# The last expert round of a sparse mixture-of-experts kernel, written out behind its loop

## The chip, the cores and the metric

The kernel is one program on one NeuronCore of a Trainium2 chip. Times are microseconds of device time for one launch; of several runs the median is taken. The engines are TensorE (PE; its weight loads are PEld), VectorE (DVE), ScalarE (ACT), GpSimd (POOL) and SyncE (SP, which here only starts DMA transfers).

## The reference

The network is a trunk of two layers on 1024 tokens of width 1024. A layer is a token mixer (a spatial gating unit in layer 0, a pooling mixer in layer 1) and a mixture of 32 experts with SwiGLU. Each token goes to two experts. Only the expert part matters here:

```python
def expert_block(args):
    xb, e = args                               # 128 gathered token rows, one expert
    hid = jax.nn.silu(xb @ w_gate[e]) * (xb @ w_up[e])
    return hid @ w_down[e]
...
w_sorted = gate.reshape(-1)[order]
out = jax.ops.segment_sum(y_sorted * w_sorted[:, None], tok, num_segments=n_tok)
```

`w_gate` and `w_up` of an expert are 1024x512, `w_down` is 512x1024, all float32.

## The kernel before

The expert part, `moe(L)` on every engine, runs once per layer over n items. An item is one expert with at most 128 of its tokens; n is read from a table in the middle of the run, and is 32 or 33 here. Every float32 operand is split in a high part (`w_hi`, `a_hi`, made by ACT with a copy) and a low part (`w_lo`, `a_lo`, made by DVE with a subtraction), and a product is three matmuls: high by high, high by low, low by high (`three`, L525 to L527).

A **round** i of the loop on PE is `round_(i)` (L744 on): the gate and up products of item i (`gate_up`, 8 units of 6 matmuls, banks 0 and 1), the 8 transposes of the token rows of item i+1 (`x_transposes`, L709, banks 4 and 5), the down product of item i-1 (`down`, 4 units of 6 matmuls, banks 2 and 3), and the 4 transposes of item i's inner rows (`h_transposes`, L742, bank 6). So the down product runs one round late. A unit is 128x1024 of weights: ACT splits it (L844), DVE makes its low part (L1154), and there are four slots for split units, each free again when PE has used it (`M.used`).

On ACT a round is: four units, the weighted rows of item i-2 out of banks 2 and 3 into `y_sb` (`y_out`, L1025), the high part of the inner rows of item i-1 (`h_split`), four units, the SiLU (L1015), four units of the down weights, and the high part of the next token rows (`x_split`). DVE follows in the same order; its `hidden` (L1504) makes SiLU(gate) times up, the input of `h_transposes`.

On POOL a round is: `gather(i+1)`, which loads the 128 list entries of the next item (`meta_g`) and gathers its token rows into `xg`; `scatter(i-2)`, which writes the weighted rows to `y_rows` in DRAM and waits until they have landed; and `load_meta(i-1)`, which loads the entries that the next `y_out` and scatter need (`meta_s`).

The loop runs to round n-1, whatever is left to gather: in its last round a spare gather and spare transposes for an item n are made, which nobody uses. Behind the loop stands the down product of the last item. It waits (L772) until ACT has emptied banks 2 and 3 of the item before, and then, in `down`, until the split inner rows are there; these are made behind that emptying on ACT. POOL then scatters item n-2, loads the entries of item n-1, and scatters it. SP waits for all scatters and gathers (L346, L347) and loads `y_rows` back, two rows per token in 8 transfers (L352). DVE adds each pair of rows to the residual (L1179, L1181) and normalizes it (L1162).

The loop of ACT and DVE starts at round 3, that of PE and POOL at round 2. The down weights of the last item are loaded early into their own place (`early_raw`, semaphore `g.last_dn`).

## Time and profile before

| what | us |
|---|---|
| median of 3 runs | 2170.41 |
| lowest, highest run | 2161.85, 2173.72 |
| span of the profiled execution | 2153.2 |
| TensorE busy in it | 2007.8 (93%) |

The span reaches from the first to the last instruction. In the views, L followed by a number is a line of the kernel; "x4" after an instruction is a count of equal ones merged; "[3.16 <-DVE a_lo L1154]" says that the engine had stood idle for 3.16 us and that the DVE instruction of L1154 ended it. A matmul of 512 columns shows as 0.39 us but the next starts 0.23 us after it, since they are pipelined.

### The profile page before, as it was taken

The page shows a single profiled execution, that of the slowest core. Times are in us where ns is not written, and L with a number is a line of the kernel's source. Part 1 is how long each engine was busy: PE and PEld are TensorE (multiplying, and loading weights), DVE is VectorE, ACT ScalarE, POOL GpSimd, SP SyncE. Part 2 cuts the span into 40 slices and gives each one's busy share as a digit, 9 for nine tenths or more (in the row PEclk, how much of TensorE's full clock was granted, in tenths as well). Part 3 has the DMA queues.
Part 4 walks back from the last instruction along what each step waited for, and adds up shares of the span by engine and source line. Part 5 has one row for each costly group of instructions (what it writes and reads, how often), then busy time and mean ns, then how long its engine had stood idle before and what let it go on. Part 6 is the DMA issues. An engine that isn't in the chain of part 4 may idle for free.

```text
span 2153.2 us, 31966 instructions
## 1 busy us (share of the span) xinstructions
PE 2007.8 (93%) x9518; PEld 1672.5 (78%) x9518; DVE 1581.8 (73%) x1894; ACT 1365.6 (63%) x1742; POOL 283.4 (13%) x319
## 2 busy tenths in 40 slices
PE   7999999999969999999999879898799999999991
PEld 6887778888858888888887658687588888888871
DVE  4335353426479999999998786757799999999985
ACT  3442244433248888888888743434588888888872
POOL 1000000000031211112222100001212222221110
PEclk9999999999979999999999979999899999999995
DMA  7332222322478999999999663144889999999976
GB/s 278 98 98 68 89 85 95 99 97 80 163 203 308 381 380 384 386 384 372 379 383 364 236 243 95 66 147 134 265 332 377 378 381 383 376 376 387 391 282 251
DMA packets 165860, 553.13 MB, mean 257 GB/s; under 512 B 31525, under 2 KB 33797, under 8 KB 163632
## 3 DMA queue, kind: packets, MB, share of 16 engines
q1 hardware_dynamic: 138624, 507.57, 64.0%
q0 software_dynamic: 25840, 39.95, 5.3%
q10 hardware_dynamic: 1344, 4.94, 0.6%
q8 instruction: 30, 0.49, 0.1%
q14 instruction: 22, 0.18, 0.0%
HBM read 539.85 MB, written 47.78 MB: 273 GB/s over the span
## 4 chain that ended last, share of the span: by engine, by line
PE 71%; DMA 14%; DVE 6%; issue 4%; ACT 2%; POOL 1%; POOLq 1%; SPq 0%; ACTq 0%; DVEq 0%
PE bank L525 22%; PE bank L527 22%; PE bank L526 22%; DMA y_rows<-big,metas 7%; DMA metas<-lists 5%; PE bank L709 2%; PE bank L584 2%; DVE big L1162 1%; DMA lists<-payload,place 1%; PE bank L742 1%; POOLq L461 1%; POOL lists L453 1%; PE bank L623 1%; PE bank L573 1%; DVE w_lo L1154 1%
## 5 line engine op out<-in xcount | busy, mean ns | idle before, releaser
L525 PE MATMUL bank<-w_hi,a_hi 128*128 128x512 f32 x1816 | 725.9, 400 | 17.6 <-DVE a_lo L1154 12.6
L1154 DVE TENSOR_TENSOR w_lo<-raw,w_hi 128x1024 fp32r<-128x1024 f32 x376 | 458.6, 1225 | 356.8 <-ACT w_hi L844 334.7
L527 PE MATMUL bank<-w_hi,a_lo 128*128 128x512 f32 x1816 | 713.6, 393 | 0.0
L526 PE MATMUL bank<-w_lo,a_hi 128*128 128x512 f32 x1816 | 711.4, 392 | 0.0
L844 ACT ACTIVATE w_hi<-raw 128x1024 fp32r<-128x1024 f32 x376 | 397.3, 1060 | 415.2 <-PE bank L527 407.9
L1154 DVE TENSOR_TENSOR w_lo<-big,w_hi 128x1024 fp32r<-128x1024 f32 x530 | 621.1, 1220 | 28.7 <-ACT w_hi L844 22.7
L844 ACT ACTIVATE w_hi<-big 128x1024 fp32r<-128x1024 f32 x530 | 548.3, 1064 | 108.0 <-PE bank L527 107.8
L525 PEld LDWEIGHTS bank<-w_hi,a_hi 128*128 128x128 f32 x1816 | 344.7, 190 | 88.7 <-issue 9.5
L527 PEld LDWEIGHTS bank<-w_hi,a_lo 128*128 128x128 f32 x1816 | 343.7, 189 | 74.7
L526 PEld LDWEIGHTS bank<-w_lo,a_hi 128*128 128x128 f32 x1816 | 344.4, 190 | 68.4
L1154 DVE TENSOR_TENSOR a_lo<-bank,a_hi 128x512 fp32r<-128x512 f32 x231 | 150.2, 685 | 54.4 <-ACT a_hi L844 54.4
L525 PE MATMUL bank<-a_hi,w_hi 128*128 128x512 f32 x416 | 162.2, 390 | 2.6 <-DVE a_lo L1154 2.6
L525 PE MATMUL bank<-w_hi,y_hi 128*128 128x512 f32 x384 | 152.3, 397 | 13.1 <-DVE y_lo L1154 5.4
L527 PE MATMUL bank<-a_hi,w_lo 128*128 128x512 f32 x416 | 161.9, 389 | 0.0
L526 PE MATMUL bank<-a_lo,w_hi 128*128 128x512 f32 x416 | 161.8, 389 | 0.0
L844 ACT ACTIVATE a_hi<-bank 128x512 fp32r<-128x512 f32 x231 | 127.5, 595 | 46.1 <-PE bank L709 34.2
L527 PE MATMUL bank<-w_hi,y_lo 128*128 128x512 f32 x384 | 150.5, 392 | 0.0
L526 PE MATMUL bank<-w_lo,y_hi 128*128 128x512 f32 x384 | 150.4, 392 | 0.0
L464 POOL DMA_INDIRECT big<-normed,metas x67 | 75.5, 1128 | 339.3 <-DMA metas<-lists 164.2
L481 POOL DMA_DIRECT2D metas<-lists x65 | 37.6, 579 | 491.2 <-issue 471.7
L1025 ACT ACTIVATE big<-bank,metas 128x512 f32<-128x512 f32 x130 | 81.5, 678 | 27.8 <-PE bank L527 17.9
L525 PEld LDWEIGHTS bank<-w_hi,y_hi 128*128 128x128 f32 x384 | 72.8, 190 | 33.2 <-issue 10.4
(160 smaller groups left out, 1646.8 us busy)
## 6 DMA issues: line engine op xcount, KB each, us to landing
big<-in_w_gate SPq DMA_DIRECT2D x260, 512.0 KB, 5.3
big<-in_w_up SPq DMA_DIRECT2D x254, 512.0 KB, 6.6
raw<-in_w_down SPq DMA_DIRECT2D x244, 512.0 KB, 6.8
raw<-in_a_w_in SPq DMA_DIRECT2D x64, 512.0 KB, 4.0
raw<-in_a_w_out SPq DMA_DIRECT2D x32, 512.0 KB, 3.2
big<-y_rows SPq DMA_DIRECT2D x16, 1024.0 KB, 7.4
big<-in_w_down SPq DMA_DIRECT2D x16, 512.0 KB, 8.8
raw<-in_b_w_in SPq DMA_DIRECT2D x16, 512.0 KB, 3.3
```

The costliest lines, as they stand in the source:

```text
L453: pool.indirect_dma_start(out=lists[L][:, :], out_offset=bass.IndirectOffsetOnAxis(ap=place[:, t, k:k + 1], axis=0), in_=payload[:, t, k, ...
L461: return pool.value_load(table[0:1, 1, bass.ds(i, 1)], min_val=0, max_val=E * BPE - 1)
L464: pool.indirect_dma_start(out=dst, out_offset=None, in_=normed[L][:, :], in_offset=bass.IndirectOffsetOnAxis(ap=metas[:, column:column + 1 ...
L481: pool.dma_start(meta_s, lst[:, bass.ds(b, 1), :].rearrange("p b w -> p (b w)")).then_inc(M.meta_s, 16)
L525: pe.matmul(dst, left_hi, right_hi, start=first, stop=False)
L526: pe.matmul(dst, left_hi, right_lo, start=False, stop=False)
L527: return pe.matmul(dst, left_lo, right_hi, start=False, stop=last)
L584: last = pe.matmul(bank[b][:, 0:LGC], xt[L][t][:, k * P:(k + 1) * P], router[:, k, :], start=k == 0, stop=k == KC - 1)
L709: last = pe.transpose(bank[4 + k // 4][:, k % 4 * P:(k % 4 + 1) * P], rows[:, k // 2, k % 2, :], ident)
L844: return nc.scalar.activation(dst, src, ACT.Copy)
L1025: nc.scalar.activation(y_sb[:, c, :], bank[2 + c][:, :], ACT.Copy, scale=meta_s[:, 2:3].bitcast(F32)).then_inc(M.y_out, 1)
L1154: return nc.vector.tensor_tensor(dst, src, f32(hi), ALU.subtract)
```

## The change

The loop ends one round earlier on PE, ACT, DVE and POOL, and the last round is written out behind it, in both layers. Six things change in it.

1. PE: the 8 transposes of the item that does not exist are left out, and ACT's and DVE's `x_split` of it.
2. POOL: `gather(n)` is left out, and SP's wait for gathers.
3. PE: the 4 transposes of the last item's inner rows move from behind the down product of item n-2 to its middle, ahead of its third unit (`ahead_of=((2, ...),)`).
4. The split inner rows of the last item get a place of their own (`end_h_hi`, `end_h_lo`, in the room of the token rows), so they can be made while the down product still reads the others.
5. The last down product goes to banks 4 and 5 and no longer waits for `y_out`. Its rows go to `end_y` (the room of `xg`) with the entries that are still in `meta_g`, so POOL neither waits for the landing of the scatter ahead of it nor loads entries again.
6. ACT and DVE take the last four units, the split of the inner rows and `y_out(n-2)` in another order.

```diff
-                with pe.Fori(2, n) as i:
+                with pe.Fori(2, n - 1) as i:
                     round_(i, lambda i: pe.wait_ge(M.y_out, 2 * (i - 1)))
-                pe.wait_ge(M.y_out, 2 * (n - 1))
-                down(n - 1, lambda j: pe.wait_ge(M.lo, ROUND * n + j + 1))
+                pe.wait_ge(M.hid, n - 1)
+                gate_up(n - 1, lambda j: pe.wait_ge(M.lo, ROUND * (n - 1) + j + 1), 0)
+                pe.wait_ge(M.y_out, 2 * (n - 2))
+                down(n - 2, lambda j: pe.wait_ge(M.lo, ROUND * (n - 1) + GU + j + 1),
+                     ahead_of=((2, lambda: h_transposes(n - 1)),))
+                down(n - 1, lambda j: pe.wait_ge(M.lo, ROUND * n + j + 1), end_h_hi, end_h_lo, 4)
...
@@ scalar
-                with act.Fori(3, n) as i:
+                with act.Fori(3, n - 1) as i:
                     round_(i, moe_raw)
-                for c in range(DN):
-                    act.wait_ge(g.last_dn, 16 * DN * (L + 1))
-                    act.wait_ge(M.used, ROUND * (n - 1) + GU + c + 1)
-                    copy(w_hi[:, c, :], early_raw[c]).then_inc(M.hi, 1)
+                round_(n - 1, moe_raw, following=False)
+                end_unit(0, n)
+                end_unit(1, n)
+                h_split(n - 1, end_h_hi)
+                end_unit(2, n)
                 y_out(n - 2, ROUND * n)
-                h_split(n - 1)
-                y_out(n - 1, ROUND * n + DN)
+                end_unit(3, n)
+                act.wait_ge(M.used, ROUND * n + DN)
+                act.wait_ge(M.meta_g, 16 * (n - FIRST))
+                weighted_rows(end_y, 4, meta_g)
...
@@ vector
-                for c in range(DN):
-                    unit(GU + c, ROUND * n + c + 1, early_down).then_inc(M.lo, 1)
-                h_split(n - 1)
+                round_(n - 1, moe_raw, following=False)
+                end_unit(0, n)
+                h_split(n - 1, end_h_lo, end_h_hi)
+                for c in range(1, DN):
+                    end_unit(c, n)
...
@@ gpsimd
-                scatter(n - 2)
-                load_meta(n - 1)
-                scatter(n - 1)
+                scatter(n - 3)
+                load_meta(n - 2)
+                scatter_rows(n - 2, meta_s, y_sb)
+                scatter_rows(n - 1, meta_g, end_y)
...
@@ sync
                 sp.wait_ge(M.scattered, 16 * n)
-                sp.wait_ge(M.gathered, 16 * n)
```

On PE, in layer 0, the end of the down product of item n-2 before the change (banks 2 and 3), the transposes of the inner rows (bank 6), the loop's branch, the two waits, and the last down product:

```order
L525 MATMUL bank3<-w_hi,a_hi 128x512
L526 MATMUL bank3<-w_lo,a_hi 128x512
L527 MATMUL bank3<-w_hi,a_lo 128x512
L742 MATMUL bank6<-cf,big 128x128 x4
L770 ISA
L770 COMPARE_AND_BRANCH
L772 ISA
L729 REGISTER_ALU
L773 ISA
L525 MATMUL bank2<-w_hi,a_hi 128x512
```

The same place after the change: the transposes stand between the second and the third unit of the down product of item n-2.

```order
L531 MATMUL bank3<-w_hi,a_hi 128x512
L532 MATMUL bank3<-w_lo,a_hi 128x512
L533 MATMUL bank3<-w_hi,a_lo 128x512
L751 MATMUL bank6<-cf,big 128x128 x4
L784 REGISTER_ALU
L531 MATMUL bank2<-w_hi,a_hi 128x512
L532 MATMUL bank2<-w_lo,a_hi 128x512
L533 MATMUL bank2<-w_hi,a_lo 128x512
```

Two units later the last down product follows, in banks 4 and 5, with one wait in front of it in place of the transposes and the wait for ACT.

On ACT, in layer 0, the written-out end before the change: four units, the rows of item n-2 (banks 2 and 3), and the inner rows (bank 6) behind them:

```order
L844 ACTIVATE w_hi<-big 128x1024
L1022 ISA
L1023 REGISTER_ALU
L1025 ACTIVATE big<-bank2,metas 128x512
L1025 ACTIVATE big<-bank3,metas 128x512
L844 ACTIVATE a_hi<-bank6 128x512
```

And after it: the inner rows stand behind the second unit, and the rows of item n-2 between the third and the fourth.

```order
L857 ACTIVATE w_hi<-big 128x1024
L1046 REGISTER_ALU
L857 ACTIVATE w_hi<-big 128x1024
L857 ACTIVATE a_hi<-bank6 128x512
L1046 REGISTER_ALU
L857 ACTIVATE w_hi<-big 128x1024
L1040 REGISTER_ALU
L1036 ACTIVATE big<-bank2,metas 128x512
L1036 ACTIVATE big<-bank3,metas 128x512
L1046 REGISTER_ALU
```

The inner rows moved ahead of two units and of the emptying of banks 2 and 3.

## Rows read from the trace of the kernel before

**Rows 1.** The page: its head and the busy time of each engine.

```profile
span 2153.2 us, 31966 instructions
PE 2007.8 (93%) x9518; PEld 1672.5 (78%) x9518; DVE 1581.8 (73%) x1894; ACT 1365.6 (63%) x1742; POOL 283.4 (13%) x319
```

**Rows 2.** Timeline of PE, end of layer 0's experts: start, length, instruction, idle before.

```profile
1214.55 1.11 PE L709 MATMUL bank<-cf,big 128*128 128x128 f32 x8
...
1220.99 0.60 PE L742 MATMUL bank<-cf,big 128*128 128x128 f32 x4
1224.74 0.79 PE L525 MATMUL bank<-w_hi,a_hi 128*128 128x512 f32 x1 [3.16 <-DVE a_lo L1154]
...
1230.02 0.63 PE L525 MATMUL bank<-w_hi,a_hi 128*128 128x512 f32 x1
...
1231.12 0.40 PE L525 MATMUL bank<-w_hi,a_hi 128*128 128x512 f32 x1
...
1232.93 0.39 PE L527 MATMUL bank<-w_hi,a_lo 128*128 128x512 f32 x1
```

**Rows 3.** Timeline of PE, end of layer 1's experts.

```profile
2090.71 1.11 PE L709 MATMUL bank<-cf,big 128*128 128x128 f32 x8
...
2097.14 0.60 PE L742 MATMUL bank<-cf,big 128*128 128x128 f32 x4
2100.90 0.49 PE L525 MATMUL bank<-w_hi,a_hi 128*128 128x512 f32 x1 [3.16 <-DVE a_lo L1154]
...
2107.87 0.39 PE L527 MATMUL bank<-w_hi,a_lo 128*128 128x512 f32 x1
```

**Rows 4.** Windows: length, busy time of each engine, granted clock, DMA share, GB/s.

```profile
1224.70:1230.40 5.70, 5.66 (x13) 4.46 (x14) 0.00 (x0) 0.00 (x0) 1.16 (x2) 0.50 0.22 87
```

**Rows 5.** Timeline of ACT, end of layer 1's experts.

```profile
2091.88 1.07 ACT L844 ACTIVATE a_hi<-bank 128x512 fp32r<-128x512 f32 x2
2093.24 1.06 ACT L844 ACTIVATE w_hi<-big 128x1024 fp32r<-128x1024 f32 x1 [0.30 <-PE bank L527]
...
2098.30 1.25 ACT L1025 ACTIVATE big<-bank,metas 128x512 f32<-128x512 f32 x2
2099.44 0.60 ACT L844 ACTIVATE a_hi<-bank 128x512 fp32r<-128x512 f32 x1
2108.37 1.27 ACT L1025 ACTIVATE big<-bank,metas 128x512 f32<-128x512 f32 x2 [8.33 <-PE bank L527]
```

**Rows 6.** Timeline of DVE, ends of the experts of layer 1.

```profile
2087.99 5.24 DVE L1154 TENSOR_TENSOR w_lo<-raw,w_hi 128x1024 fp32r<-128x1024 f32 x4
2093.14 0.68 DVE L1504 TENSOR_TENSOR big<-bank,big 128x512 f32<-128x512 f32 x1
...
2094.94 4.72 DVE L1154 TENSOR_TENSOR w_lo<-big,w_hi 128x1024 fp32r<-128x1024 f32 x4
2100.07 0.69 DVE L1154 TENSOR_TENSOR a_lo<-bank,a_hi 128x512 fp32r<-128x512 f32 x1 [0.42 <-ACT a_hi L844]
```

**Rows 7.** Timeline of DVE, the last inner rows of layer 0.

```profile
1216.98 0.68 DVE L1504 TENSOR_TENSOR big<-bank,big 128x512 f32<-128x512 f32 x1
```

**Rows 8.** Timelines of POOL and of SP's queue, end of layer 1's experts.

```profile
2083.26 1.03 POOL L486 DMA_INDIRECT y_rows<-big,metas  x1 [0.31 <-issue]
2090.37 0.58 POOL L481 DMA_DIRECT2D metas<-lists  x1 [6.08 <-issue]
...
2110.52 0.99 POOL L486 DMA_INDIRECT y_rows<-big,metas  x1 [4.86 <-ACT big L1025]
...
2113.78 18.25 SPq L352 DMA_DIRECT2D big<-y_rows  x8
```

**Rows 9.** The page, DMA issues: count, size of each, median us to landing.

```profile
metas<-lists POOLq DMA_DIRECT2D x128, 2.0 KB, 4.9
```

**Rows 10.** Timeline of PE, a short wait before inner-row transposes in layer 0.

```profile
646.50 0.66 PE L742 MATMUL bank<-cf,big 128*128 128x128 f32 x4 [1.04 <-DVE big L1504]
...
647.45 0.39 PE L527 MATMUL bank<-w_hi,a_lo 128*128 128x512 f32 x1
```

56 lines of the change are left out of this document (37 added, 19 removed).

## The prediction

> **What bounds the kernel now.** I read the page first: PE is busy for 93% of the span [rows 1], so whatever shortens PE's stream or closes one of its gaps shortens the run, unless something else is right behind. Then I read PE's timeline over the two places that the change touches, the ends of the experts of layer 0 and layer 1. Both look alike. PE makes 8 spare transposes, the down product of item n-2 (24 matmuls), 4 transposes, and then stands still for 3.16 us until DVE has made the low part of the inner rows [rows 2, 3]. After that gap the last down product does not run at full pace: in layer 0 its matmuls show 0.63 us instead of 0.39 until 1230.02 [rows 2], and the granted clock of that stretch is 0.50 [rows 4], the level of 1.2 GHz in place of 2.4.
>
> Behind the last matmul everything is a chain with nothing beside it: ACT weights the rows 0.11 us later, POOL starts the scatter, SP starts the loads 3.26 us after that [rows 5, 8], and DVE adds and normalizes. In layer 0 the same chain leads into the next mixer. So the end of PE's last down product moves the rest of the run one for one, in each layer. That is the quantity to work out.
>
> **Pace.** From 1231.12 to 1232.93 lie 8 matmul starts, 0.226 us each [rows 2]. A down product of 24 matmuls is then 5.5 us (24 x 0.226, and 0.1 for the first behind a transpose), and the last matmul ends 0.16 us later than the next would start.
>
> **Part 1, spare transposes.** From their start to the start of the inner-row transposes are 6.44 us in layer 0 and 6.43 in layer 1 [rows 2, 3]. With 5.5 for the product, the transposes hold PE for 0.9 us. All of it is on the path: 0.9 per layer. ACT's and DVE's two splits of these rows go too (1.07 us on ACT [rows 5]); they only make room.
>
> **Part 2, the gap.** It is made of a queue on ACT: the last unit, then the emptying of banks 2 and 3 (2098.30, 1.25 us), then the inner rows' high part (2099.44), then DVE's low part, which starts at 2100.07 and takes 0.69 [rows 5, 6]. After the change PE does not wait for the emptying, since it has other banks, and the inner rows are split while PE still works. The gap of 3.16 goes if nothing else is late, so I put the new order on a time axis for layer 1, from the old start of the spare transposes, 2090.71.
>
> - PE: units 0 and 1 of the down product of item n-2 end at about 2093.6 (12 x 0.226, and 0.16). The transposes now need `hidden`, which DVE ends at 2093.82 [rows 6]: 2093.14 and 0.68. It can't come earlier, since its place is behind the four units that DVE takes back to back from 2087.99. So the change adds a wait of about 0.3 us, and behind it stand the third and fourth unit and the last product. In the kernel before this wait is hidden by the two other units. In layer 0 DVE ends `hidden` at 1217.66 [rows 7], and PE is ready at 1214.55 + 2.87 = 1217.4: 0.3 again.
> - PE: transposes 2093.9, third unit 2094.3, last down product from 2097.1, its units at 2098.5, 2099.9 and 2101.2, end 2102.8.
> - ACT: units 0 and 1 by 2094.7, inner rows to 2095.3, unit 2 (free when PE has used the third unit, 2095.9) to 2097.0, emptying of banks 2 and 3 from 2097.4 to 2098.7, unit 3 to 2099.7. These use 1.06, 0.60 and 1.25 us [rows 5].
> - DVE: unit 0 to 2095.0, inner rows to 2096.0 (needed at 2097.1), unit 1 to 2097.2, unit 2 to 2098.4, unit 3 to about 2101.0, needed at 2101.2. This is the narrowest place, 0.2 us; if it misses, it costs some tenths. From both sides: 0 and 0.5 us per layer. I take 0, because every other unit comes over 0.9 us early.
>
> Sum of part 2: 3.16 - 0.3 = 2.9 per layer.
>
> **Part 3, the clock.** The last down product takes 1224.74 to 1233.32 in layer 0, 8.6 us, and 2100.90 to 2108.26 in layer 1, 7.4 us [rows 2, 3], against 5.7 at full pace. If PE never stands for long, 2.9 and 1.7 us come back. Would the 0.3 us wait and the four transposes lower the clock instead? The trace has a harder case: a wait of 1.04 us right before the same four transposes, and the matmuls behind them still show 0.39 us [rows 10]. So I take the full gain. The Trainium skill says otherwise of transposes ("TensorE: Matmul & The Clock Gate", "Part 4: PE-mode transpose"): they don't count as work for the clock as matmuls do. By that rule the wait and the transposes are one hole, and a hole in the middle of the down product could set the clock down; the row just named speaks against it.
>
> **Part 4, POOL, SP and ACT behind it.** The second scatter no longer waits for the landing of the first nor for its entries. Before, ACT's last weighting started 0.11 us behind PE, so this chain had not been late; taking it away gives 0 by itself. But an earlier end of PE would have made it late: with the old order the entries of the last item are asked for only when the scatter of item n-2 has landed, which took 7.1 us in the busy stretch (2083.26 to 2090.37 [rows 8]), and they take up to 4.9 more [rows 9]; counted from a scatter at 2099.6 that can reach past 2102.8, where PE now ends. This part protects the gain. Is the first scatter ready? The emptying needs the entries of item n-2, which POOL asks for at 2090.37 at the latest [rows 8]; with the median landing of 4.9 us [rows 9] they are there at 2095.3, before 2097.4. POOL's first scatter starts near 2099.6 and takes 1 us; the second is due at 2105.1 (0.11, 1.27 and 0.88 us behind PE's end, as before [rows 5, 8]). Nothing queues. The spare gather of layer 1 stands just ahead of the scatter at 2083.26; leaving it out can only bring that scatter forward. SP's wait for gathers was over long before; 0.
>
> **Sum.** Layer 0: 0.9 + 2.9 + 2.9 = 6.7. Layer 1: 0.9 + 2.9 + 1.7 = 5.5. Together 12.2 us of a span of 2153.2, so the profile should show about 2141. The runs' median is 2170.4, 17.2 above the span shown; a saving in the middle and at the end of the program is the same in both, so I forecast 2158.2.
>
> **The rivals.**
>
> *The clock falls inside the product.* Wait and transposes set the clock down, and the slow matmuls only move from the last product to the stretch around it. Then part 3 gives nothing: 0.9 + 2.9, twice, is 7.6 us, 2162.8. For it: both gaps of 3.16 us were followed by slow matmuls, and this is the only change of kind that PE's stream gets. Against it: [rows 10]. The rule of the Trainium skill above, of the same page and section, would lead here. Chance 0.15.
>
> *The new order is late elsewhere.* ACT's unit 3 or a split misses its time, or the layers behind the experts don't follow one for one (PE restarts in the next mixer at another point of its clock's history). From the places above a miss costs 1 to 3 us per layer; the gain is then 6 to 10 us, about 2162. Chance 0.17.
>
> *Slower: instructions don't come in time.* The written-out round adds 86 rows to PE's program in each layer (172 in both), and 26 or 27 to ACT's and DVE's. The program leaves its loop while the DMA queues are busy, and at a place where PE has no wait to hide a late fetch; before, PE left the loop into its 3.16 us gap. Price: the trace doesn't show a fetch stall, the nearest row is a small transfer in that stretch, 4.9 us [rows 9]. One such stall per layer, with the slow clock behind it (2.9), costs 15.6 and leaves 3.4 slower, 2173.8; it decides from 6 us per layer. Two per layer give 2189. Against it: ACT leaves its loop behind the splits at 2091.88 and takes the next unit at 2093.24, with only 0.30 us of idle time, which ends with PE's matmul [rows 5], though by then the weights had landed and the queues were free; and DVE goes from `hidden` to the next units without a stop [rows 6]. Chance 0.06, of which 0.04 beyond 0.5%.
>
> **How the numbers follow.** My forecast has 0.62. A measurement of this kernel can tell about 0.5%, 10.9 us, from no change. The forecast of 12.2 lies just above it, so of its 0.62 I give 0.50 to faster and 0.12 to within 0.5%; of the rivals of 2162 to 2163 the runs' spread brings 0.04 to faster and leaves 0.28 within. Faster 0.54, same 0.42, slower 0.04. The range: upward the cases at 2163 and 5 us for the spread of runs (2161.9 to 2173.7 for the kernel before), 2168. Downward, the last products can have been wholly slow in other executions (24 matmuls at 0.2 us more are 4.8, so 1.9 and 3.1 more than in this one): 5 us more gain, 2153, and 3 for the spread, 2150.
>
> **What would show it.** Right: in both layers the down product of item n-2 directly behind the gate and up products, the four transposes in its middle behind a wait of 0.2 to 0.5 us, the last product without a gap at 0.39 us per matmul, ACT's last weighting about 12 us behind the start of the down product of item n-2, two scatters about 5 us apart, span about 2141. Wrong: matmuls of 0.63 us behind the moved transposes, a gap of PE ahead of the last unit, idle time of "issue" on PE just behind the loop, or a chain from the last weighting to the first load longer than the 5.4 us of before (2108.37 to 2113.78).

## The result, and the profile after

| | before | after |
|---|---|---|
| median, us | 2161.85 (9 runs) | 2149.40 (9 runs) |
| lowest, highest, us | 2153.86, 2173.72 | 2141.00, 2158.45 |
| span of the profiled execution, us | 2153.2 | 2156.5 |

The ratio of after to before is 0.9934, with an interval of 0.9909 to 0.996: about 14 us less (8.6 to 19.7); the two medians are 12.5 apart. The forecast gain of 12.2 us lies inside that interval. The forecast time of 2158.2 is 8.8 us above the measured one, and the forecast range began at 2150.0, 0.6 us above it. The profile was forecast at about 2141 us and shows 2156.5.

The two profiled executions alone would say that the change made the kernel 3.3 us slower. So the places that were changed have to be read apart from the rest.

**The changed places.** The timeline of PE (TensorE) over the end of layer 0's experts, in the kernel after. The columns are start, length, instruction, idle time before it and what ended it. L531 to L533 are the three matmul lines that were L525 to L527, L751 makes the inner-row transposes, L1529 is `hidden`; further down L857 is ACT's split (L844 before), L1036 its weighting and emptying (L1025), L1179 DVE's low parts (L1154), L488 the scatter, L483 and L466 the entries' load and the gather:

```profile
1227.32 0.39 PE L533 MATMUL bank<-w_hi,a_lo 128*128 128x512 f32 x1
1228.01 0.66 PE L751 MATMUL bank<-cf,big 128*128 128x128 f32 x4 [0.29 <-DVE big L1529]
1228.42 0.47 PE L531 MATMUL bank<-w_hi,a_hi 128*128 128x512 f32 x1
1228.73 0.39 PE L532 MATMUL bank<-w_lo,a_hi 128*128 128x512 f32 x1
...
1236.48 0.39 PE L533 MATMUL bank<-w_hi,a_lo 128*128 128x512 f32 x1
```

The transposes stand in the middle of the down product of item n-2 behind a wait of 0.29 us, where [rows 2] had a gap of 3.16 us behind them. No matmul between the two ends of this fence shows more than 0.47 us. The same in layer 1, against [rows 3]:

```profile
2102.83 0.66 PE L751 MATMUL bank<-cf,big 128*128 128x128 f32 x4 [0.29 <-DVE big L1529]
...
2111.30 0.39 PE L533 MATMUL bank<-w_hi,a_lo 128*128 128x512 f32 x1
```

The windows over both stretches (length, busy time of PE, its weight loads, DVE, ACT and POOL, granted clock, DMA share, GB/s) show the clock at 1.00, the level of 2.4 GHz, where [rows 4] had 0.50:

```profile
1228.00:1237.00 9.00, 8.86 (x40) 7.07 (x40) 5.36 (x5) 4.67 (x7) 0.99 (x1) 1.00 0.75 288
2102.80:2111.80 9.00, 8.85 (x40) 7.07 (x40) 5.38 (x5) 4.67 (x7) 0.98 (x1) 1.00 0.13 53
```

From here on the **tail** of a layer is the stretch from the start of what stands right behind the last gate and up products to the end of the last matmul. Before, it took 18.8 us in layer 0 (1214.55 to 1232.93 and 0.39 [rows 2]) and 17.6 in layer 1 [rows 3]. After, it takes 12.0 in both: the twelve matmuls ahead of the wait are 2.5 us (they start at 1224.83 and 2099.66, 11 x 0.226 ahead of the last of them), and the last ends at 1236.87 and 2111.69. That is 6.7 and 5.5 us less.

ACT, DVE, POOL and SP's queue behind it, layer 1, one timeline each. ACT:

```profile
2103.54 0.58 ACT L857 ACTIVATE a_hi<-bank 128x512 fp32r<-128x512 f32 x1
2104.92 1.06 ACT L857 ACTIVATE w_hi<-big 128x1024 fp32r<-128x1024 f32 x1 [0.80 <-PE bank L533]
2106.28 1.27 ACT L1036 ACTIVATE big<-bank,metas 128x512 f32<-128x512 f32 x2 [0.30 <-PE bank L533]
2107.44 1.06 ACT L857 ACTIVATE w_hi<-big 128x1024 fp32r<-128x1024 f32 x1
2111.72 1.26 ACT L1036 ACTIVATE big<-bank,metas 128x512 f32<-128x512 f32 x2 [3.23 <-PE bank L533]
```

DVE:

```profile
2102.09 0.68 DVE L1529 TENSOR_TENSOR big<-bank,big 128x512 f32<-128x512 f32 x1
...
2104.15 0.69 DVE L1179 TENSOR_TENSOR a_lo<-bank,a_hi 128x512 fp32r<-128x512 f32 x1 [0.25 <-ACT a_hi L857]
...
2108.53 1.23 DVE L1179 TENSOR_TENSOR w_lo<-big,w_hi 128x1024 fp32r<-128x1024 f32 x1 [1.29 <-ACT w_hi L857]
```

POOL:

```profile
2108.43 0.98 POOL L488 DMA_INDIRECT y_rows<-big,metas  x1 [10.26 <-ACT big L1036]
2114.21 0.98 POOL L488 DMA_INDIRECT y_rows<-big,metas  x1 [4.79 <-issue]
```

SP's queue:

```profile
2117.47 7.69 SPq L354 DMA_DIRECT2D big<-y_rows  x5
```

On the time axis of the prediction (after minus 8.95 us, so that both begin at 2090.71) the steps stand like this:

| layer 1 | forecast | measured |
|---|---|---|
| transposes | 2093.9 | 2093.88 |
| emptying of banks 2 and 3, start (2106.28) | 2097.4 | 2097.33 |
| last down product, start (2106.08) | 2097.1 | 2097.13 |
| first scatter | 2099.6 | 2099.48 |
| unit 3 ready on DVE (2109.76) | 2101.0 | 2100.81 |
| unit 3 needed by PE (2110.16) | 2101.2 | 2101.21 |
| end of PE | 2102.8 | 2102.74 |
| second scatter | 2105.1 | 2105.26 |

The narrowest place had 0.4 us to spare instead of 0.2.

**Where the 12.2 us went in this pair of executions.** PE's timeline of after has these gaps in the last rounds of layer 0:

```profile
1137.03 0.50 PE L531 MATMUL bank<-w_hi,a_hi 128*128 128x512 f32 x1 [2.19 <-DVE w_lo L1179]
...
1157.37 0.80 PE L531 MATMUL bank<-w_hi,a_hi 128*128 128x512 f32 x1 [2.26 <-DVE w_lo L1179]
...
1184.70 1.22 PE L715 MATMUL bank<-cf,big 128*128 128x128 f32 x8 [1.92 <-DMA big<-normed,metas]
```

Behind DVE stands ACT, and ACT stands for the list entries of the item whose rows it must weight (4 numbers per token, among them the weight). ACT's timeline:

```profile
1133.02 1.26 ACT L1036 ACTIVATE big<-bank,metas 128x512 f32<-128x512 f32 x2 [2.94 <-DMA metas<-lists]
1153.36 1.27 ACT L1036 ACTIVATE big<-bank,metas 128x512 f32<-128x512 f32 x2 [3.00 <-DMA metas<-lists]
```

And behind ACT stands POOL, which asks for these entries at 1128.31 and 1148.15, each time 8 us after it was last busy. POOL's timeline:

```profile
1128.31 0.57 POOL L483 DMA_DIRECT2D metas<-lists  x1 [8.47 <-issue]
...
1136.13 1.76 POOL L466 DMA_INDIRECT big<-normed,metas  x1 [5.45 <-DMA metas<-lists]
1138.20 1.96 POOL L488 DMA_INDIRECT y_rows<-big,metas  x1 [0.30 <-issue]
1148.15 0.58 POOL L483 DMA_DIRECT2D metas<-lists  x1 [8.00 <-issue]
```

The kernel before has the same sort of gap in layer 0. It stood in the trace that I had before me, and the rows that I took from it do not show it:

```profile
1171.76 0.50 PE L525 MATMUL bank<-w_hi,a_hi 128*128 128x512 f32 x1 [2.13 <-DVE w_lo L1154]
```

In its middle rounds (all but the first two of a layer and the tail) such gaps sum to 5.1 us (0.41, 0.21, 2.13 and 2.38); in after's to 11.2 (2.19, 2.26, 1.92, 0.19, 2.06, 0.52 and 2.08). With five of the seven gaps of about 2 us come 7 or 8 slow matmuls (0.57 to 0.80 us in place of 0.39), with the 2.19 and the 1.92 none. The product of item n-2 begins 10.3 us later than before in layer 0 (1224.83 to 1214.55). The tail gives 6.7 and 0.1 back. Before's first load behind it is

```profile
1238.74 10.04 SPq L352 DMA_DIRECT2D big<-y_rows  x6
```

and after's starts at 1242.19. From there to the product of item n-2 in layer 1 are 857.5 us in place of 852.0, 5.5 more; the tail takes 5.5 less, its chain to SP 0.3 more, and what follows 0.4 less. 10.3 - 6.8 + 5.5 - 5.5 + 0.3 - 0.4 = 3.4, the difference of the spans but for rounding.

A part of the 5.5 between the layers comes from the mixer of layer 1, where nothing was changed. PE has a gap of 2.58 us there in both kernels. In the profiled execution of after 14 matmuls of 0.63 us or more follow it, and the granted clock is 0.61 from 1359.1 to 1367.1; in before (1355.05) and in a second execution of after (`after_again` below) none does, at a clock of 1.00. PE's timelines of after and of `after_again`:

```profile
1359.07 0.76 PE L531 MATMUL bank<-a_hi,w_hi 128*128 128x512 f32 x1 [2.58 <-DVE a_lo L1179]
```

```profile
1358.60 0.47 PE L531 MATMUL bank<-a_hi,w_hi 128*128 128x512 f32 x1 [2.58 <-DVE a_lo L1179]
```

That costs the one execution 2.9 us (13.2 or 13.3 us in the others from this gap to PE's next wait of 2.07 us, and 16.1 here). None of the added time lies where code was changed. Whether the rest is the change's doing or that of the execution is what the second half of the experiments asks.

### The profile page after: what moved, and what is told of

Read it like the earlier page. It is cut to its first block, busy times and chain, and to the rows that moved or that the text cites. A ratio compares the mean times of both kernels' runs of the same rounds, so it can differ in the third digit from the quotient of the medians.

```text
span 2156.5 us, 31848 instructions
## 1 busy us (share of the span) xinstructions
PE 2011.2 (93%) x9502; PEld 1672.1 (78%) x9502; DVE 1576.6 (73%) x1890; ACT 1363.8 (63%) x1738; POOL 283.2 (13%) x313
## 4 chain that ended last, share of the span: by engine, by line
PE 63%; DMA 20%; DVE 6%; issue 6%; POOLq 2%; POOL 2%; ACT 2%; SPq 0%; ACTq 0%; DVEq 0%
PE bank L531 19%; PE bank L533 19%; PE bank L532 19%; DMA y_rows<-big,metas 11%; DMA metas<-lists 7%; PE bank L715 1%; PE bank L590 1%; POOLq L463 1%; DMA lists<-payload,place 1%; DVE big L1187 1%; POOL big L466 1%; POOL lists L455 1%; PE bank L629 1%; PE bank L751 1%; DMA big<-normed,metas 1%
## 5 line engine op out<-in xcount | busy, mean ns | idle before, releaser
L531 PE MATMUL bank<-w_hi,a_hi 128*128 128x512 f32 x1816 | 725.6, 400 | 15.7 <-DVE w_lo L1179 9.3
L533 PE MATMUL bank<-w_hi,a_lo 128*128 128x512 f32 x1816 | 712.6, 392 | 0.0
L1179 DVE TENSOR_TENSOR w_lo<-raw,w_hi 128x1024 fp32r<-128x1024 f32 x376 | 456.8, 1223 | 349.1 <-ACT w_hi L857 329.6
L857 ACT ACTIVATE w_hi<-raw 128x1024 fp32r<-128x1024 f32 x376 | 397.4, 1060 | 418.3 <-PE bank L533 410.8
L1179 DVE TENSOR_TENSOR w_lo<-big,w_hi 128x1024 fp32r<-128x1024 f32 x530 | 621.0, 1219 | 32.7 <-ACT w_hi L857 24.9
L857 ACT ACTIVATE w_hi<-big 128x1024 fp32r<-128x1024 f32 x530 | 546.9, 1063 | 105.5 <-PE bank L533 103.9
L531 PEld LDWEIGHTS bank<-w_hi,a_hi 128*128 128x128 f32 x1816 | 344.1, 189 | 88.5 <-DVE w_lo L1179 13.7
L533 PEld LDWEIGHTS bank<-w_hi,a_lo 128*128 128x128 f32 x1816 | 342.9, 189 | 74.5
L1179 DVE TENSOR_TENSOR a_lo<-bank,a_hi 128x512 fp32r<-128x512 f32 x227 | 147.5, 683 | 70.5 <-ACT a_hi L857 63.4
L531 PE MATMUL bank<-a_hi,w_hi 128*128 128x512 f32 x416 | 163.7, 394 | 2.6 <-DVE a_lo L1179 2.6
L533 PE MATMUL bank<-a_hi,w_lo 128*128 128x512 f32 x416 | 163.0, 392 | 0.0
L531 PE MATMUL bank<-w_hi,y_hi 128*128 128x512 f32 x384 | 154.2, 402 | 9.4 <-DVE y_lo L1179 3.9
L857 ACT ACTIVATE a_hi<-bank 128x512 fp32r<-128x512 f32 x227 | 125.2, 596 | 52.1 <-PE bank L715 39.6
L533 PE MATMUL bank<-w_hi,y_lo 128*128 128x512 f32 x384 | 152.5, 397 | 0.0
L466 POOL DMA_INDIRECT big<-normed,metas x65 | 74.3, 1142 | 321.9 <-DMA metas<-lists 158.7
L488 POOL DMA_INDIRECT y_rows<-big,metas x65 | 90.5, 1392 | 76.3 <-ACT big L1036 54.4
L483 POOL DMA_DIRECT2D metas<-lists x63 | 36.1, 573 | 482.4 <-issue 462.0
L1036 ACT ACTIVATE big<-bank,metas 128x512 f32<-128x512 f32 x130 | 81.6, 679 | 27.7 <-DMA metas<-lists 19.7
```

Of the source, the lines that this page charges most:

```text
L466: pool.indirect_dma_start(out=dst, out_offset=None, in_=normed[L][:, :], in_offset=bass.IndirectOffsetOnAxis(ap=metas[:, column:column + 1 ...
L483: pool.dma_start(meta_s, lst[:, bass.ds(b, 1), :].rearrange("p b w -> p (b w)")).then_inc(M.meta_s, 16)
L488: pool.indirect_dma_start(out=y_rows[L][:, :], out_offset=bass.IndirectOffsetOnAxis(ap=meta[:, 1:2], axis=0), in_=rows.rearrange("p n f -> ...
L531: pe.matmul(dst, left_hi, right_hi, start=first, stop=False)
L533: return pe.matmul(dst, left_lo, right_hi, start=False, stop=last)
L857: return nc.scalar.activation(dst, src, ACT.Copy)
```

## The experiments on the change

Each of the first five takes back one part of the change, and each is judged by its own stretch, from the start of the product of item n-2 (or of what stands ahead of it) to the end of PE, since the rounds ahead differ from execution to execution by more than what was undone. Each ran once; their times, 2148.2 to 2157.6 us, cannot rank them.

**Spare transposes back** (`a1_spare`).

```diff
                 gate_up(n - 1, lambda j: pe.wait_ge(M.lo, ROUND * (n - 1) + j + 1), 0)
+                rows = xg.rearrange("t (q p k) -> t q k p", p=P, k=2)
+                for k in range(KC):
+                    pe.transpose(bank[4 + k // 4][:, k % 4 * P:(k % 4 + 1) * P], rows[:, k // 2, k % 2, :], ident)
```

> The changed kernel with the 8 spare transposes put back in the last round, on TensorE alone (their result is used by nobody; no gather and no splits for them). Read in each layer: the stretch from the last matmul of the gate and up products to the end of the last matmul, 12.0 us in the changed kernel's trace. My theory: 0.9 us for the transposes, less the 0.3 us wait for the inner rows that they hide, so 12.6 us and no wait ahead of the inner-row transposes. Rival (a transpose costs its shown 1.11 us and hides nothing): 13.1 us.

PE's timeline in layer 1 (L785 are the added transposes):

```profile
2092.12 1.11 PE L785 MATMUL bank<-cf,big 128*128 128x128 f32 x8
...
2095.84 0.60 PE L751 MATMUL bank<-cf,big 128*128 128x128 f32 x4
...
2104.26 0.39 PE L533 MATMUL bank<-w_hi,a_lo 128*128 128x512 f32 x1
```

From 2092.12 to 2104.65 are 12.5 us, against 12.0. Eight transposes hold PE for 0.9 us, but 0.3 of it is the time that PE would have waited for `hidden`: the inner-row transposes now have no wait. So beside the new order this part is worth 0.5 to 0.6 us per layer, and not 0.9; the sum of both parts stays what it was, since the prediction had taken the 0.3 off part 2.

**Inner-row transposes behind the product** (`a2_behind`).

```diff
                 down(n - 2, lambda j: pe.wait_ge(M.lo, ROUND * (n - 1) + GU + j + 1),
-                     ahead_of=((2, lambda: h_transposes(n - 1)),))
+                     )
+                h_transposes(n - 1)
```

> The changed kernel with the four inner-row transposes behind the down product again, all else as changed. My theory: the wait of 0.3 us goes, but TensorE must then wait for ScalarE's and VectorE's halves of the inner rows (0.6 and 0.7 us) with nothing to do: a gap of about 1.4 us, no clock loss, and the stretch from the gate and up products to the last matmul's end is 13.2 us instead of 12.0. Rival: a gap of 1.4 us already lowers the clock (matmuls of 0.63 us behind it), 15 to 16 us.

```profile
2095.34 0.49 PE L531 MATMUL bank<-w_hi,a_hi 128*128 128x512 f32 x1 [1.49 <-DVE a_lo L1180]
```

The row is of PE's timeline. The gap is 1.49 us in both layers. The last product lasts from 2095.34 to 2101.07, 5.7 us, full pace, and the whole stretch 13.3. So with banks and buffers of its own the split alone costs 1.5 us where it isn't hidden, about half of the old 3.16; the other half, 1.67, is put down to the emptying of banks 2 and 3 ahead of it on ACT (1.25 us [rows 5]) with the waits around it. And a gap of 1.49 us does not bring the slow clock, where one of 3.16 did.

**Entries and scatters as before** (`a3_entries`).

```diff
-                scatter_rows(n - 2, meta_s, y_sb)
-                scatter_rows(n - 1, meta_g, end_y)
+                scatter(n - 2)
+                load_meta(n - 1)
+                scatter_rows(n - 1, meta_s, end_y)
...
-                act.wait_ge(M.meta_g, 16 * (n - FIRST))
-                weighted_rows(end_y, 4, meta_g)
+                act.wait_ge(M.meta_s, 16 * n)
+                weighted_rows(end_y, 4, meta_s)
```

> The changed kernel with GpSimd's end as before: it waits until the scatter of the last but one item has landed, loads the entries again, and ScalarE's last weighting needs those. TensorE's stretch stays 12.0 us. My theory: the weighting is held until about 3.3 us later than in the changed kernel (4.7 us from the scatter's start to the load, 1.9 us for the load), in each layer, and the start of the loads of y_rows with it, so this part was needed for half of what the change gives. Rival (the old chain was never on the path): the weighting starts 0.1 us behind the last matmul all the same.

PE's last matmul starts at 2107.44. ACT's timeline:

```profile
2111.20 1.26 ACT L1037 ACTIVATE big<-bank,metas 128x512 f32<-128x512 f32 x2 [6.55 <-DMA metas<-lists]
```

ACT weights the last rows 3.4 us after PE's end (2107.83), and waits for entries, not for PE; in layer 0 too (1232.11, behind a wait of 6.64 us for the entries). In the kernel after it starts 0.03 us behind PE. So this part, worth nothing by itself, keeps 3.4 us per layer of the others' gain.

**Last product in banks 2 and 3** (`a4_banks`).

```diff
-                down(n - 1, lambda j: pe.wait_ge(M.lo, ROUND * n + j + 1), end_h_hi, end_h_lo, 4)
+                pe.wait_ge(M.y_out, 2 * (n - 1))
+                down(n - 1, lambda j: pe.wait_ge(M.lo, ROUND * n + j + 1), end_h_hi, end_h_lo, 2)
...
-                weighted_rows(end_y, 4, meta_g)
+                weighted_rows(end_y, 2, meta_g)
```

> The changed kernel with the last down product in banks 2 and 3 again, behind a wait for the weighted rows of the item before. My theory: a gap of about 1.5 us (0.1 and 1.25 us for the weighting, 0.1 us to start), the stretch 13.5 us instead of 12.0. Rival: the clock falls in that gap as it did behind 3.16 us, and the stretch is over 15 us.

```profile
2098.23 0.49 PE L531 MATMUL bank<-w_hi,a_hi 128*128 128x512 f32 x1 [1.43 <-ACT big L1037]
```

PE's timeline again: 1.43 us, ended by ACT's emptying, in both layers, and full pace behind it. The end of PE comes later by more than the gap shows, since the last matmul ahead of it no longer overlaps the next (0.16 us) and the first behind it is slower to be followed (0.1): the tail is 13.76 us in layer 1 and 13.78 in layer 0, against 12.03. The banks are worth 1.7 us per layer, where I had expected 1.5.

**`hidden` one unit earlier** (`a5_hidden`), which takes away the wait that the change adds.

```diff
                     for c in range(4, ROUND):
+                        if c == ROUND - 1 and not following:
+                            hidden(i)
                         unit(c, ROUND * i + c + 1, slots if c < GU else down_slots).then_inc(M.lo, 1)
-                    hidden(i)
+                    if following:
+                        hidden(i)
```

> The changed kernel with VectorE's product for the inner rows ahead of the fourth down unit in the written-out round, not behind it. My theory: the 0.3 us wait ahead of the moved transposes goes in both layers and the stretch is 11.7 us instead of 12.0. Rival: the fourth unit comes 0.7 us later, and TensorE waits for that instead.

```profile
2095.53 0.60 PE L751 MATMUL bank<-cf,big 128*128 128x128 f32 x4
```

The wait of 0.29 us is gone, and the stretch is 11.7 us. The 0.3 us were the whole price of the new order, as the sum had them.

## The experiments on the spread

The five kernels above showed spans of 2145.9 to 2155.7 us, in an order that has nothing to do with what was undone in them: `a2_behind`, whose tails are 1.3 us longer than after's, was 10.6 us shorter than after as a whole. So something else in an execution moves 10 us. From the rows above my theory was that list entries come late. POOL's round is a chain: it issues the scatter of item i-2, waits for it to land, reads the next block number from the table, asks for the entries (into the buffer that the scatter has only then finished with), asks for the entries of the next gather, waits for these, issues the gather, and then the next scatter. POOL's timeline of the kernel before, two rounds:

```profile
900.67 1.18 POOL L486 DMA_INDIRECT y_rows<-big,metas  x1 [0.30 <-issue]
909.17 0.58 POOL L481 DMA_DIRECT2D metas<-lists  x1 [7.32 <-issue]
...
916.68 1.04 POOL L464 DMA_INDIRECT big<-normed,metas  x1 [5.14 <-DMA metas<-lists]
918.02 1.18 POOL L486 DMA_INDIRECT y_rows<-big,metas  x1 [0.30 <-issue]
```

From scatter to scatter are 17.35 us here, and neither scatter waited for ACT: both follow the gather at once. PE's round is 17.8 us (eight transposes to eight transposes, 1195.65 to 1213.46 in `b_early` below). This is one of POOL's shorter rounds: the 23 from 704.24 to 1114.74 in the same trace take 17.1 to 19.2 us, 17.85 in the mean, and none of their scatters waited for ACT. So the chain has no reserve in its round; what it is ahead of PE at the start is all it has. A landing of 5 us for the gather's entries and one of about 7 for the scatter lie in it. In the profiled execution of after the longest of these rounds come at the end of layer 0 (five of 18.9 to 21.1 us, from 1097.36 to 1197.50), where the gaps are. The rival: the added time came with the change (its longer program, the moved round), and would stay.

**Entries copied from a block loaded one round earlier** (`v_shift` on after, `b_shift` on before). The edit in its core:

```diff
+        meta_1, meta_2 = cols[:, 16:20].bitcast(I32), cols[:, 20:24].bitcast(I32)
...
+                def next_meta(i, inc):
+                    pool.tensor_copy(meta_s, meta_2).then_inc(M.meta_s, inc)
+                    pool.wait_ge(M.meta_s, 4 * i + 15)
+                    waited()
...
                 with pool.Fori(2, n - 1) as i:
+                    waited()
+                    pool.tensor_copy(meta_1, meta_g).then_inc(M.meta_s, 1)
+                    pool.wait_ge(M.meta_s, 4 * i + 9)
+                    waited()
                     gather(i + 1)
                     scatter(i - 2)
-                    load_meta(i - 1)
+                    next_meta(i - 1, 2)
+                    pool.tensor_copy(meta_2, meta_1).then_inc(M.meta_s, 1)
+                    pool.wait_ge(M.meta_s, 4 * i + 12)
+                    waited()
```

> The changed kernel, and in all rounds GpSimd no longer loads each item's list entries a second time: the entries that came for the gather are handed on by three small copies on GpSimd (from the gather's place over two others to the one that the weighting and the scatter read), so behind the landing of a scatter there is a copy where there was a load of 5 us and the 3 us ahead of it. It asks where the 12 to 20 us between executions of one kernel come from. My theory: from late entries. The traces of before and after show ScalarE waiting for them by 2.8 to 3.1 us in 2 and 4 rounds, each followed by about 2.1 us of TensorE idle and some 10 slow matmuls. Then this kernel has no TensorE gap over 0.5 us in the middle of the experts, runs at 2135 to 2142 us, and its runs differ by under 6 us. Rival: the transfers are too slow as such (weights, gather, scatter share the queues), and the lateness moves to the gather or to the weights; then time and spread stay as in the changed kernel, 2141 to 2158.

> The kernel before with the same handing-on of the entries by copies, and nothing else. By my theory its runs lie close together too, at about 2150, and the distance to the changed kernel with these copies is the effect of the written-out round without the noise: 12 us (6.7 in layer 0 and 5.5 in layer 1, 1 to 2 us to either side for the slow matmuls behind the gap). Rival: with the noise gone the distance is under 9 us, as if part of the gain had come from elsewhere.

Both missed. `v_shift` took 2205.38 us (ratio 1.0188, 1.0142 to 1.0234), `b_shift` 2217.14 (1.0233, 1.0179 to 1.0286). What I had wanted came: the ACT group of the weighting (L1054) stands for entries no more, only 7.2 us for PE. But POOL's timeline of `v_shift` shows

```profile
905.60 0.18 POOL L487 COPY metas<-cols 128x4 int32<-128x4 int32 x1 [6.33 <-DMA y_rows<-big,metas]
...
914.79 1.03 POOL L467 DMA_INDIRECT big<-normed,metas  x1 [4.67 <-DMA metas<-lists]
916.13 2.08 POOL L494 DMA_INDIRECT y_rows<-big,metas  x1 [0.30 <-issue]
925.00 0.18 POOL L487 COPY metas<-cols 128x4 int32<-128x4 int32 x1 [6.80 <-DMA y_rows<-big,metas]
```

Here 19.4 us pass from copy to copy, more than PE's 17.8: the three copies and their waits stand between the landing of the scatter and the request for the next gather's entries (905.60 to 909.54, 3.9 us), and the request comes no earlier than before. PE then waits for the gather (the place that the rival named, at a higher price), as the page's group of PE's transposes shows (busy time, mean ns, idle time before them):

```profile
L733 PE MATMUL bank<-cf,big 128*128 128x128 f32 x520 | 81.1, 304 | 61.9 <-DMA big<-normed,metas 61.7
```

In the steady stretch from 670 to 1190 us PE is busy for 497.7 of 520 us, where before had 517.3 and after 513.5. So the entries of the weighting were moved off the chain, and the chain itself was made longer. The miss is the first sign that POOL's round bounds the kernel once it passes PE's: PE lost 22 us in the 29 rounds of that stretch, 0.8 per round, and the kernels became 38 us (`v_shift`) and 49 us (`b_shift`) slower than the 2167.79 us of before (11 runs) beside them.

**The same with `hidden` earlier** (`v_shift_hid`), `a5_hidden`'s edit on `v_shift`:

```diff
+                        if c == ROUND - 1 and not following:
+                            hidden(i)
```

> Both: the entries handed on by copies and the inner rows' product ahead of the fourth unit. Expected 0.6 us below the kernel with the copies alone, too little to be told by time; by the trace 11.7 us instead of 12.0 in the stretch. With it the kernel is about 1% below the kernel before, if the theory on the entries holds; within 0.2% of the changed kernel by the rival.

2202.5 us (1.018, 1.0135 to 1.0225), against 2205.38: nothing that this comparison can tell, as the runs of the two spread over 29 and 31 us. In its trace the inner-row transposes of both last rounds (1243.69 and 2144.39) have no wait, as in `a5_hidden`. The "1% below the kernel before" fell with the theory of the copies.

**Both loads right behind the issue of the scatter** (`w_early` on after, `b_early` on before). The entries of the next weighting go to a block of their own, and are copied to where ACT reads when the scatter has landed; the entries of the gather are asked for as soon as the last gather has landed, not behind the scatter's landing. One copy instead of three:

```diff
+        meta_next = cols[:, 16:20].bitcast(I32)
...
+                def scatter_round(j, then):
+                    scatter_rows(j, meta_s, y_sb, 0)
+                    load_meta(j, meta_next)
+                    if then is not None:
+                        then()
+                    pool.wait_ge(M.meta_s, 16 * (j + 1))
+                    waited()
+                    pool.wait_ge(M.scattered, 16 * j)
+                    waited()
+                    pool.tensor_copy(meta_s, meta_next).then_inc(M.row_full, 1)
+                    pool.wait_ge(M.row_full, j + 1)
+                    waited()
...
                 with pool.Fori(2, n - 1) as i:
-                    gather(i + 1)
-                    scatter(i - 2)
-                    load_meta(i - 1)
+                    pool_round(i, i - 1, True)
```

> The changed kernel with GpSimd's round taken out of its chain of waits. In the kernel with the copies GpSimd ran one thing after another: landing of the scatter (7 to 8 us), three copies with their waits (2 to 3), load of the next gather's entries (5), gather and scatter issue (2.5), 18 to 19 us in all, where TensorE's round is 17.8; ScalarE never waited for entries, but TensorE waited 22 times for the gather. Here, right behind the issue of a scatter, the entries of the next weighting are loaded into a place of their own and those of the gather after next into the gather's, all while the scatter travels; one copy of 0.2 us follows its landing. My theory (late entries make the spread and a part of the time, and the copies failed only by GpSimd's own round): GpSimd's round is then 12 us, no wait of ScalarE for entries, no TensorE gap over 0.5 us between the third round and the last, 2135 to 2142 us and runs within 6 us of each other. Rival: the queues are too full as such, and weights, gather or scatter come late instead; time 2141 to 2158 as with the changed kernel.

> The kernel before with the same order on GpSimd, all else as before. By my theory the distance to the changed kernel with that order is 12 us (6.7 and 5.5 in the one trace of before, give or take 1 to 2 for the slow matmuls), now with little noise on it: about 2147 to 2154 us. Rival: under 9 us.

| | median, us | lowest to highest | runs | ratio to before | span shown |
|---|---|---|---|---|---|
| before | 2167.45 | 2159.05 to 2177.63, and one of 2192.44 | 17 | | |
| `b_early` | 2150.50 | 2148.30 to 2155.54 | 6 | 0.9929 (0.9902 to 0.9957) | 2146.6 |
| after, once more (`after_again`) | 2154.43 | 2144.55 to 2173.38 | 10 | 0.9955 (0.9926 to 0.9984) | 2150.9 |
| `w_early` | 2135.82 | 2134.36 to 2137.34 | 5 | 0.9857 (0.9829 to 0.9886) | 2132.4 |

POOL's timeline of `w_early`:

```profile
899.97 1.03 POOL L516 DMA_INDIRECT y_rows<-big,metas  x1 [6.33 <-ACT big L1065]
901.02 0.58 POOL L511 DMA_DIRECT2D cols<-lists  x1
...
906.02 0.49 POOL L505 COPY metas<-cols 128x4 int32<-128x4 int32 x1 [3.05 <-DMA cols<-lists]
...
917.76 1.03 POOL L516 DMA_INDIRECT y_rows<-big,metas  x1 [6.34 <-ACT big L1065]
```

The requests travel while the scatter does, in place of one wait after another, and POOL waits 6.3 us for ACT in almost every round: that is its reserve, where it had none. Its own work is then 11.5 us of the round (I had expected 12), and the round is PE's, 17.8 us. ACT waits for entries nowhere, PE has no gap over 0.5 us between the third round and the tail, and time and spread are in the expected ranges. In the windows PE is never idle in the steady stretch (before 517.25, after 513.52, `after_again` 510.09):

```profile
670.00:1190.00 520.00, 520.00 (x2454) 434.22 (x2453) 486.76 (x468) 450.30 (x527) 115.57 (x147) 1.00 0.98 378
```

The spread between executions falls from 19 us (before, 16 of its 17 runs) and 29 us (after) to 7 (`b_early`) and 3 (`w_early`). The new kernels ran fewer times, but no five of after's ten runs lie within 3 us of each other, and of all choices of six from the 16 of before only 4% lie within 7.2. So most of the spread hung on POOL's chain, in the kernel before as in the kernel after. Which of the two moved requests did it isn't shown: no run moves one alone. The rival, that the lost time came with the change, has little left: `w_early` has the change and lost nothing, and `a2_behind`, with the written-out round too, reaches the tail of layer 0 at 1213.2 us, ahead of before's 1214.55. That the change makes POOL's lateness somewhat worse is not excluded (after's spread is the wider one here).

With that noise gone the pair `b_early` and `w_early` measures the change most cleanly: 2150.50 to 2135.82, 14.7 us, and 11 at the least (2148.30 to 2137.34), since the runs do not overlap. Not all of it is the change's. The spans differ by 2146.6 - 2132.4 = 14.2: 2.9 up to the product of item n-2 in layer 0 (part of it a wait of 1.59 us for a gather at 661.53, and 0.9 of a longer one for the first gather, both in `b_early` only and both ahead of what was changed), 5.5 in each tail, and 0.3 for the rest. So 11.0 lie where code was changed, just inside the 12 (give or take 1 to 2) that I had expected, and outside its rival of under 9. The tails of `b_early` are 17.5 us in both layers; its gap in layer 1, in PE's timeline,

```profile
2094.73 0.49 PE L552 MATMUL bank<-w_hi,a_hi 128*128 128x512 f32 x1 [3.15 <-DVE a_lo L1184]
```

has slow matmuls behind it that cost 1.7 us, and so has that of layer 0; in `b_shift`, whose tails are those of before, both gaps (3.16 and 3.15 us) cost 1.7 as well. In `w_early` the tails are 12.0:

```profile
2079.11 0.66 PE L780 MATMUL bank<-cf,big 128*128 128x128 f32 x4 [0.29 <-DVE big L1561]
...
2087.58 0.39 PE L562 MATMUL bank<-w_hi,a_lo 128*128 128x512 f32 x1
```

**The kernel after, once more** (`after_again`), no edit.

> The changed kernel itself, once more, beside the others. It gives a second execution of the same program: its stretch from the gate and up products to the last matmul should be 12.0 us in both layers again, and where its span differs from the first one's (2156.5 us), TensorE's idle time and slow matmuls in the middle rounds should differ by as much, behind rounds in which ScalarE waited over 2.5 us for entries.

Its tails are as in the first profile (12.0 us, waits of 0.29 and 0.30). Its middle rounds have gaps of 1.07, 1.08, 1.24, 6.53 and 2.35 us, 12.3 in all. Their sizes are other than the first time, but all except the first (886.67) they stand in the same rounds: 1137.34, 1156.71 and 1181.32 in layer 0, against 1137.03, 1157.37 and 1184.70, and 2068.88 in layer 1, one round ahead of the tail, against 2074.61. Before's larger ones (1171.76 and 2065.69) stand there too. Why the last rounds of a layer are the ones isn't shown.

The second half of the expectation missed. This span is 5.6 us shorter than the first, while the gaps of the middle rounds with their slow matmuls cost the same within half a us (some 16 us each, at 0.2 for a slow one); both executions end layer 0's experts at 1236.9. The difference lies behind: 4.8 us from there to PE's first instruction behind the choice of experts in layer 1 (275.3 us, against 270.5; before has 272.9), 2.9 of them the slow matmuls behind the 2.58 us gap shown above, and 1.0 in the experts of layer 1. So the clock in the mixer is a second source of spread, and the account of POOL's chain doesn't cover it. The profiled executions of `b_early` and `w_early` (272.9 and 273.0) had no slow matmuls behind it.

## Why the prediction was right, and where it failed

**What bounds the kernel**: right for the two tails, incomplete for the rest. PE's 93% and its timeline at the ends showed what a shorter tail would give. I did not ask what else was as long as PE's 17.8 us round in the middle, and the answer was in the trace: POOL's scatter without a wait for ACT, in nearly every round.

**Part 1, spare transposes, 0.9 per layer**: the size holds (12.5 with them against 11.7 without them and without the wait: 0.8). `a1_spare` adds that beside the new order a third of it is hidden, since the transposes would fill the 0.3 us wait.

**Part 2, the gap, 2.9 per layer**: right, with the 0.3 that it adds (measured 0.29 twice). Three edits under it were tested apart. Moving the transposes is worth 1.3 (`a2_behind`), the banks 1.7 (`a4_banks`); `hidden` costs 0.3 (`a5_hidden`).

**Part 3, the clock, 2.9 and 1.7**: right in this pair, 1.00 granted in both stretches. The first term is less firm than it looked. Of the six last products behind such a gap in the traces (before, `b_early`, `b_shift`, two layers each) five lost 1.7 us, and only the one in layer 0 of before lost 2.9. So the loss behind a gap of 3.16 us differs between executions, and 1.7 was the better value for both; the sum would have been 11.0.

**The rule on transposes.** Four transposes behind a wait of 0.29 us, in the middle of the product, left the matmuls behind them at 0.39 us; in `a2_behind` four transposes and then 1.49 us of standing still did too. The Trainium skill ("TensorE: Matmul & The Clock Gate", "Part 4: PE-mode transpose") has it that transposes don't count as work for the clock as matmuls do; by that rule a product cut in this way is at risk. No run of this case shows such a loss, and the rival with the chance of 0.15 that came from it did not come true.

**Part 4, the entries**: right in both halves. Zero by itself, and without it the last weighting is 3.4 us late (`a3_entries`). The two times that I took from the busy stretch were too long for this place, where the DMA share is 0.06 to 0.22: from the scatter's start to the request 4.6 us (2104.59 to 2109.21) in place of 7.1, and 2.0 for the entries (2109.21 to 2111.20) in place of 4.9, which is a median and not the most that it can be.

**The rivals**: nothing was late elsewhere in the tails, and no instruction came late there: the transposes and the last product follow the loop without a wait of "issue". One of my own signs of being wrong did appear: in layer 1 the chain from the last weighting to the first load is 5.75 us (2111.72 to 2117.47), where before had 5.41. It cost 0.3 us. What lies behind the experts did not follow one for one in the profiled pair (2.4 us more), but not by the change, as the second execution of after shows.

**The sum** (6.7 and 5.5) was measured as 6.7 and 5.5 in the profiled pair, and as 5.5 and 5.5 in the pair `b_early` and `w_early`. The mechanism of the gain was right and its size good to about 1 us.

**The step that failed is the last of the sum**: "The runs' median is 2170.4, 17.2 above the span shown". I read 17.2 us as a distance between the span and the time, and carried it over. But a run's time is only 1.6 to 2.9 us above its own span (after: 2158.45 to 2156.5, 2141.0 to 2139.3; the kernel before: 2159.05 to 2157.3, 2192.44 to 2190.7). The span of 2153.2 belonged to one of the fastest executions, and the rest of the 17.2 was spread between executions, of which three runs give a poor median: the nine beside the kernel after gave 2161.85, 8.6 us lower. With that one the same gain gives 2161.85 - 12.2 = 2149.7, 0.3 from what was measured. That close an agreement is luck: the measured gain is known to some 5 us only, and two other comparisons put the kernel before at 2167.79 (11 runs) and 2167.45 (17). By the same step the span was forecast at about 2141, as if the next profiled execution had to be as fast a one; it was a slow one, 2156.5, and another execution of after had 2139.3. The range failed by the same step: 5 us for the spread on one side and 3 on the other, where the three times (2161.9 to 2173.7) already lay 12 us apart, and the span shown, with some 2 us on top, said that 2155 was possible as well. A lower end of 2143 (2155 - 12) would have followed from it.

**What stays open.** Which landing is late in a given execution, and why, isn't shown, only that the reserve decides whether PE notices. Why the same gap of 2.58 us in the mixer brings the slow clock in one execution and not in another isn't either. And in layer 1 of the kernel after, the second scatter starts 1.23 us behind ACT's end (2112.98 to 2114.21), where it was 0.88 before and 0.87 in layer 0; 0.3 us that nothing in the trace names.

## What to carry to other kernels

Read a time against its own span before you carry a gain from a profile to a median: if the distance isn't the small one that every run has (here 1.6 to 2.9 us), the rest is spread, and it has a place in the program. Find that place by asking, for each engine with a long chain of small transfers and waits in its round, whether its last step waits for the engine that should bound the round; where it doesn't, that chain may have no reserve, and moving its requests ahead of its waits can gain more (17 and 19 us here, in the one kernel and the other) than the tail that one was polishing. And move the requests, not the data: three copies put into that chain cost 38 and 49 us. When profiles of single executions are compared, a slow clock behind one gap can be 3 us of the difference.

## What was not expected of the hardware

- The clock's answer to a gap is not a matter of its length alone. At 1.00 over the 9 us behind it: gaps of 1.08, 1.24, 1.92, 2.19 (after, 1137.03), 2.34 (`a5_hidden`, 2068.86) and 2.64 us (`a2_behind`, 1172.04), and at 1.00 over the product behind them 1.43 and 1.49. Partly at the lower level: 2.06 (after, 1217.67: 0.81), 2.13 (before, 1171.76) and 2.26 us (after, 1157.37), both 0.82, and 6.53 (0.71). One gap of 2.58 us in the mixer, the same in each execution, was followed by 0.61 over 8 us in one and by 1.00 in the others. Behind 3.16 us in layer 0 the last product lost 2.9 us in one execution and 1.7 in two.
- A POOL copy of 128x4 numbers takes 0.18 us in one place and 1.19 in another (905.60 and 905.94 in `v_shift`); three of them with their waits and the load's issue held the chain for 3.9 us.
- The landing of a 2 KB load of entries did not have to become shorter: 4.9 us in the median before [rows 9], 5.0 at most in the round of `w_early` shown (901.02 to 906.02), at a DMA share of 0.98. At the ends of the layers, with the share at 0.06 to 0.21, the same load is there after 2.0 us (`a3_entries`, 1230.10 to 1232.11 and 2109.21 to 2111.20).
